# Gate sums from two rounded parts, a per-unit wait in the last stage, and extra products at the third norm

## What is computed

```python
def gla_chunk_scan(q, k, v, log_a, s0):
    def step(s, blk):
        qb, kb, vb, gb = blk
        b = jnp.cumsum(gb, axis=2)          # sums of the tokens' gates
        q_dec = qb * jnp.exp(b)
        att = jnp.where(tri, jnp.einsum('bhtd,bhsd->bhts', q_dec, kb * jnp.exp(-b)), 0.0)
...
log_a = jax.nn.log_sigmoid(z.astype(jnp.float32)) / GLA_TAU
...
h_lat = h_lat + mod_l[2] * o_lat
h_lat = h_lat + mod_l[5] * sqrelu_mlp(modulate(rmsnorm(h_lat, norm2_g[i]), mod_l[3], mod_l[4]),
                                      mlp_w1[i], mlp_w2[i])
...
return rmsnorm(h_lat, final_g)
```

## Time and profile before

| | us |
|---|---|
| executions of the kernel before | 971.64, 972.18, 976.74 |
| their median | 972.18 |
| the profiled execution | 975.54 |
| its span in the profile | 973.7 |
| PE busy / DVE busy / ACT busy | 951.2 / 795.6 / 554.4 |
| mean granted clock of PE, of full speed | 0.994 |

### The profile page before, as it was taken

How to read it: one execution, slowest core, us unless ns; L and a number is a source line. 1 busy time by engine, 2 the same in 40 slices (tenths; PEclk the granted TensorE clock), 3 DMA queues, 4 the chain that set the end, 5 groups by cost and what they waited for, 6 DMA issues and landing times.

```text
span 973.7 us, 20548 instructions
## 1 busy us (share of the span) xinstructions
PE 951.2 (98%) x7196; PEld 913.9 (94%) x7196; DVE 795.6 (82%) x1308; ACT 554.4 (57%) x893; POOL 1.2 (0%) x6
## 2 busy tenths in 40 slices
PE   8999999999999999999999999999999899999996
PEld 7999999999999899999999998888899899998885
DVE  6988899998989789899998987855868777776553
ACT  7445666666455674766666555876533466564432
POOL 0000000000000000000000000000000000000000
PEclk9999999999999999999999999999999989999999
DMA  8876575557767464555557765554673447676651
GB/s 318 271 242 216 171 250 192 189 197 252 258 227 229 161 213 144 184 189 180 182 184 258 241 241 189 183 205 135 228 250 124 136 144 233 225 232 221 193 174 43
DMA packets 53878, 197.27 MB, mean 203 GB/s; under 512 B 5982, under 2 KB 6110, under 8 KB 53696
## 3 DMA queue, kind: packets, MB, share of 16 engines
q1 hardware_dynamic: 53680, 195.49, 60.4%
q10 hardware_dynamic: 144, 1.05, 0.3%
HBM read 195.46 MB, written 1.05 MB: 202 GB/s over the span
## 4 chain that ended last, share of the span: by engine, by line
PE 88%; DVE 7%; ACT 2%; issue 1%; DMA 1%; DVEq 0%; SPq 0%; ACTq 0%
PE ps L474 23%; PE ps L469 20%; PE ps L470 20%; PE ps L473 6%; DVE wlo L1391 3%; PE ps L502 2%; PE ps L504 2%; PE ps L503 2%; ACT whi L894 1%; PE ps L584 1%; PE ps L585 1%; PE ps L586 1%; PE ps L714 1%; PE ps L518 1%; PE ps L450 1%
## 5 line engine op out<-in xcount | busy, mean ns | idle before, releaser
L1391 DVE TENSOR_TENSOR wlo<-raw,whi 128x1024 fp32r<-128x1024 f32 x306 | 370.1, 1219 | 75.5 <-ACT whi L894 74.7
L894 ACT ACTIVATE whi<-raw 128x1024 fp32r<-128x1024 f32 x306 | 320.4, 1053 | 98.4 <-DMA raw<-stream 48.2
L469 PE MATMUL ps<-xhi,whi 128*128 128x256 f32 x1288 | 365.3, 284 | 2.5 <-DVE wlo L1391 0.9
L474 PE MATMUL ps<-xhi,wlo 128*128 128x256 f32 x1288 | 362.6, 281 | 0.0
L470 PE MATMUL ps<-xlo,whi 128*128 128x256 f32 x1288 | 362.6, 281 | 0.0
L469 PEld LDWEIGHTS ps<-xhi,whi 128*128 128x128 f32 x1288 | 244.2, 190 | 4.2 <-DVE wlo L1391 1.5
L470 PEld LDWEIGHTS ps<-xlo,whi 128*128 128x128 f32 x1288 | 244.2, 190 | 0.7 <-issue 0.5
L474 PEld LDWEIGHTS ps<-xhi,wlo 128*128 128x128 f32 x1288 | 244.2, 190 | 0.0
L469 PE MATMUL ps<-yhi,whi 128*128 128x256 f32 x400 | 112.7, 282 | 0.9 <-DVE wlo L1391 0.9
L470 PE MATMUL ps<-ylo,whi 128*128 128x256 f32 x400 | 112.4, 281 | 0.0
L474 PE MATMUL ps<-yhi,wlo 128*128 128x256 f32 x400 | 112.4, 281 | 0.0
(11 more groups left out here) (296 smaller groups left out, 1376.2 us busy)
## 6 DMA issues: line engine op xcount, KB each, us to landing
raw<-stream SPq DMA_DIRECT2D x346, 512.0 KB, 4.1
side<-stream SPq DMA_DIRECT2D x16, 512.0 KB, 4.8
h<-xT SPq DMA_DIRECT2D x2, 512.0 KB, 5.1
c<-ctxT ACTq DMA_DIRECT2D x1, 1024.0 KB, 7.3
ct<-cst SPq DMA_DIRECT2D x1, 962.5 KB, 10.0
rt_tab<-rot SPq DMA_DIRECT2D x1, 896.0 KB
cr<-crow SPq DMA_DIRECT2D x1, 512.0 KB, 7.2
state<-crow SPq DMA_DIRECT2D x1, 512.0 KB, 8.0
```

The source lines that it names most:

```text
L469: pe.matmul(dst, whi[:, w], at(hi, k), start=(k == 0), stop=False)
L474: last = pe.matmul(dst, wlo[:, w], at(hi, k), start=False, stop=(k == K - 1))
L894: c.sig(act.activation(whi[:, s * D:(s + 1) * D], raw[:, r * D:(r + 1) * D], ACT.Copy), hi_ready)
L1391: c.sig(dve.tensor_tensor(wlo[:, w], raw[:, r], whi[:, w], ALU.subtract), slots_done)
```

## The change

- `softplus` of the tokens makes three DVE operations for each direction in place of one: the sum into `za[d]`, its rounded copy `zhi_g[d]` (float32r), and the remainder `zlo_g[d]`. The one of the context stays.
- DVE makes rounded copies of the triangles and of the two-column tables (`sums_r`), once, after the context's `softplus`. All of them are 0, 1 or -1.
- `exponents` makes, instead of each plain float32 product, two float32r products, one with `zhi_g` and one with `zlo_g`, that add up in the same bank.
- In the loop of `mlp_down`, `slot_of_next_unit` counts back from the positions of the second pass: the wait is exact from the second pass on, and in the first pass the first three units wait for one position more than their own.
- `keep_warm(n)` issues n products of `zhi` with itself into bank 5, which nothing reads: 8 ahead of the third norm's column sums (with a wait for bank 5's last reader), 14 behind `spread`.

The new buffers lie over others that are unused at that time.

```diff
@@ -265,18 +265,28 @@
         za = [sb(f"za{d}", GH * T, F32, early) for d in range(2)]
         zm = [sb(f"zm{d}", GH * T, F32, early) for d in range(2)]
         early.close()
+        early = ExitStack()
+        sb("early_held", DC * T + 2 * GH * T, F32, early)
+        zhi_g = [sb(f"zhi_g{d}", GH * T, F32R, early) for d in range(2)]
+        early.close()
         E1 = sb("E1", 2 * GH * T, F32, stage)
         E = [sb("E0", 2 * GH * T, F32, stage), E1]
         qf = [sb(f"qf{d}", GH * T, F32, stage) for d in range(2)]
         gq = sb("gq", GH * T, F32, stage)
         gk = sb("gk", GH * T, F32, stage)
         gv = sb("gv", 2 * D, F32, stage)
+        early = ExitStack()
+        zlo_g = [sb(f"zlo_g{d}", GH * T, F32R, early) for d in range(2)]
+        early.close()
         rsil = sb("rsil", DC * T, F32, stage)
         ki = [sb(f"ki{d}", GH * T, F32, stage) for d in range(2)]
         kz = [sb(f"kz{d}", GH * T, F32, stage) for d in range(2)]
         ck = sb("ck", GH * T, F32, stage)
         kt = sb("kt", GH * T, F32, stage)
         cval = sb("cval", 2 * D, F32, stage)
+        early = ExitStack()
+        sums_r = sb("sums_r", 6 * P + 4, F32R, early)
+        early.close()
         att = sb("att", 2 * 4 * P, F32, stage)
         att_b = sb("att_b", 2 * P, F32, stage)
         osq = sb("osq", 4 * T, F32, stage)
@@ -428,7 +438,10 @@
 
             def slot_of_next_unit():
                 u = c.n.get("unit", 0)
-                pos, step = c.position(u, c.per.get("unit", 0))
+                per = c.per.get("unit", 0)
+                pos, step = c.position(u, per)
+                if per and u >= PHASE_AT["mlp_down"]:
+                    pos, step = POS[u + per] - per, per
                 pe.wait_ge(slots_done, c.i * step + (pos + 1) if step else pos + 1)
                 c.n["unit"] = u + 1
                 return u % RING
@@ -708,15 +721,19 @@
                     pe.wait_ge(ev("expo_read"), n - 2)
                 else:
                     pe.wait_ge(ev("gate_bank_read"), 6)
-                sums = cst_of("sums_b" if d else "sums_f")
+                parts = zhi_g[d], zlo_g[d]
                 for b in range(2):
-                    gates = zm[d][:, b * 512 + m * P:b * 512 + (m + 1) * P]
-                    pe.matmul(ps[5 + n % 3][:, b * T:(b + 1) * T], gates, sums[:, b * P:(b + 2) * P], start=True, stop=True)
-                gates = zm[d][:, d * 512 + m * P:d * 512 + (m + 1) * P]
+                    sums = sums_r[:, (3 * d + b) * P:(3 * d + b + 2) * P]
+                    for i, part in enumerate(parts):
+                        gates = part[:, b * 512 + m * P:b * 512 + (m + 1) * P]
+                        pe.matmul(ps[5 + n % 3][:, b * T:(b + 1) * T], gates, sums, start=(i == 0), stop=(i == 1))
                 if d:
                     pe.wait_ge(ev("factors"), 1)
-                pe.matmul(STAT[:, T + 2 * n:T + 2 * n + 2], gates, cst_of("halves")[:, 2 * d:2 * d + 2], start=True, stop=True)\
-                    .then_inc(ev("expo"), 1)
+                for i, part in enumerate(parts):
+                    gates = part[:, d * 512 + m * P:d * 512 + (m + 1) * P]
+                    last = pe.matmul(STAT[:, T + 2 * n:T + 2 * n + 2], gates, sums_r[:, 6 * P + 2 * d:6 * P + 2 * d + 2],
+                                     start=(i == 0), stop=(i == 1))
+                last.then_inc(ev("expo"), 1)
 
             def ctx_state(d):
                 pe.wait_ge(ev("ctx_keys"), d + 1)
@@ -852,11 +869,19 @@
             gla_out_chunks(2, 4)
             gla_out_chunks(4, 6)
             gla_out_chunks(6, DC)
+            def keep_warm(n):
+
+                for _ in range(n):
+                    pe.matmul(ps[5][:, 0:T], zhi[:, 0:P], zhi[:, 0:T], start=True, stop=True)
+
             units(DC - 3, DC, zhi, zlo)
+            pe.wait_ge(ev("gla_read"), GH)
+            keep_warm(8)
             c.take(ssum_ready, 7)
             pe.wait_ge(ev("n2_square"), 1)
             column_stat_of([ssum[:, 0:T], at(sq, 1)])
             spread()
+            keep_warm(14)
             units(MC, DC, xhi, xlo, chunks=x_ready)
             c.take(y_ready, MC - LATE)
             c.n["y_ready"] += LATE
@@ -1853,7 +1878,12 @@
 
                 i = 2 * n + d
                 dve.wait_ge(ev("gate_ln"), i + 1)
-                dve.tensor_tensor(zm[d][:, :], zm[d][:, :], za[d][:, :], ALU.add).then_inc(ev("softplus"), 1)
+                if n == 0:
+                    dve.tensor_tensor(zm[d][:, :], zm[d][:, :], za[d][:, :], ALU.add).then_inc(ev("softplus"), 1)
+                    return
+                link(dve.tensor_tensor(za[d][:, :], zm[d][:, :], za[d][:, :], ALU.add))
+                link(dve.tensor_copy(zhi_g[d][:, :], za[d][:, :]))
+                dve.tensor_tensor(zlo_g[d][:, :], za[d][:, :], zhi_g[d][:, :], ALU.subtract).then_inc(ev("softplus"), 1)
 
             def ctx_keys(d):
 
@@ -1923,6 +1953,9 @@
                     gate_in_lo(1, 3)
             softplus(0, 0)
             softplus(0, 1)
+            for k, name in enumerate(("sums_f", "sums_b")):
+                dve.tensor_copy(sums_r[:, 3 * k * P:3 * (k + 1) * P], cst_of(name))
+            link(dve.tensor_copy(sums_r[:, 6 * P:6 * P + 4], cst_of("halves")))
             for n in range(2):
                 lo_and_dots(1)
                 final_norm(6 + n)
```

## The result

The changed kernel took 966.82 us (median of 6 runs, 965.41 to 968.77), beside 971.91 us for the kernel before (6 runs, 970.27 to 976.74). The ratio is 0.9949, with a 95% interval of 0.9931 to 0.9968: 0.5% faster. The forecast was 966.5 us, in a range of 963.5 to 970.5. The profiled execution of the changed kernel took 967.01 us, with a span of 965.0 us, against 975.54 and 973.7 before.

The account below looks back on a forecast made before the run. PE was taken to bound the kernel, busy 951.2 of 973.7 us. Gate sums 2.2, third norm 1.9 and last stage 1.6 sum to 5.7 us, taking the median 972.18 to 966.5, range 963.5 to 970.5.

Parts of the forecast that it names:

- The step from the profile's sum to the median: Whole kernel: the profiled execution lies 3.4 us above the median, unexplained, so 5.7 us come off the median 972.18 too.
- Gate sums, PE's work: Eight calls of `exponents`: each falls from 1.05 to 0.61 us, so PE's work shrinks by 3.55 us.
- Gate sums, DVE: Softplus of the tokens: sum 1.22, cast 0.72, subtraction 1.22 us per direction; PE's first call starts 0.6 us later.
- Gate sums, ACT: Fourth call: PE stands 0.85 us for ACT, whose table load follows its wait for direction 1; 2.2 us gained overall.
- The tables: Three casts after the context's softplus, at most 0.5 + 0.5 + 0.2 us, cost nothing; without cover 1.2.
- The third norm: Unread products around sums and spread keep the clock at 2.4 GHz: 1.9 us gained, plus or minus 0.25.
- The last stage: Exact wait in `mlp_down`: 1.6 us gained in the last pass; first-pass loss between 0 and 0.1, taken as 0.
- the gates give little: Rival at the gate sums: DVE and ACT bound there, gain 0.6 to 1.2 instead of 2.2, 968 us; chance 0.17.
- the clock falls anyway: Rival at the third norm: PE cold, 14 products take 3.0 us, gain 0.2 instead of 1.9, 968.2 us; chance 0.13.
- the cast is slow: Rival at the gate sums: a cast takes 7 us, PE stands for it, 979.1 us, slower than before; chance 0.03.
- the wait is moved to the first pass: Rival in `mlp_down`: the first pass pays what the last one saves, 968.1 us; chance 0.05.

Follow-up runs that it names:

- undo_gates: The changed kernel with the plain float32 products and one-step softplus of before, without the table casts: 969.0 us, ratio 0.995 to the kernel before.
- before_again: The kernel before, unchanged, run again for a second profile: 972.82 us for one run, beside 973.75 (11 runs).
- undo_warm: The changed kernel without its 22 unread products: 969.33 us (10 runs), ratio 0.9958 to the kernel before.
- warm8_only: The changed kernel without the 14 unread products behind the spread, keeping the 8 ahead of the column sums: 971.97 us, one run.
- warm14_only: The changed kernel without the 8 unread products ahead of the column sums, keeping the 14 behind the spread: 972.61 us, one run.

## Why the prediction was right, and where it was wrong

**The whole.** 5.7 us were forecast. The two pairs of profiles show 5.96 and 5.70 us at the three places, and no new wait but the 0.1 us at the start of `mlp_down`. Between medians it is 5.1 and 4.6 us. The forecast for the median, 966.5, came close to the 966.82 of the first comparison, and 969.11 in the second shows how much of that is luck. The step from the profile's sum to the median, that nothing in an execution explains why it lies above or below, holds for the two profiles of each kernel: they differ mainly by the distance between products in stages that the change doesn't touch.

**Gate sums, PE's work.** Forecast 0.61 us a call, 3.55 saved. The eight calls take 5.43 us in all (11.96 less 5.78 for V6 and V7 and 0.75 ahead of the first), 0.68 each, so 8.43 - 5.43 = 3.00 us are saved. The small products themselves cost little more than the 0.12 us assumed for the two (0.14 us, 657.68 to 657.82). What was put at nothing is the first full product behind them: its successor comes 0.20 us later (657.82 to 658.02) instead of 0.12, in the five calls that follow another call. In the first call, behind its wait, it is 0.22.

**Gate sums, DVE.** Forecast 0.72 us for the cast, 0.69 measured. The extrapolation from one-source operations of 128 and 256 elements held at 1024. The first call waits 0.52 us, forecast 0.6. The table casts took 0.36, 0.36 and 0.17 us (at most 0.5, 0.5 and 0.2).

**Gate sums, ACT: the failed step.** Forecast was a wait of 0.85 us at the fourth call, since the first `decays` "waits for direction 1: 662.1, signal 0.1, then the table load of 1.28 us, which stood behind this wait". It doesn't stand behind it. In the rows before, load and exponential followed one another, and the wait ahead of the load was for PE's call, because direction 1 had long been ready; they could not tell where a later wait for direction 1 would fall. In the changed kernel the load is done during that wait, direction 1 is in use at 660.20, two exponentials are over some 0.9 us later, 661.1, and the fourth call at 662.02 needs nothing. Two smaller slips are in the same passage: it takes V6 at 2.8 us, where its own row gives 2.89, so that the wait would be some 0.8; and the terms listed for ACT add up to 664.35, not 664.5. So the forecast of 2.2 us came about by two errors of opposite sign: 0.55 too much saved on PE, and a wait of 0.8 that wasn't there. That it lies near the measured 2.48, which is 3.00 less 0.52, is luck in part.

**The tables** were free, as forecast: the three casts take 0.7 us together (624.22 to 624.93), and PE waits for nothing between 622 and 656 us.

**The third norm.** Forecast 1.9 us: 0.26 from the spread and what follows it, the rest from products at full clock. Measured 1.88, with 0.25 and 1.64. The clock stays at 2.4 GHz, the 14 end 0.17 us ahead of the first chunk (forecast 0.1), and the chunks of `xlo` set the pace. The Trainium skill ("TensorE: Matmul & The Clock Gate", Part 1) has the moment of the rise vary by half a microsecond between runs, by which I gave the term plus or minus 0.25. The runs agree on the size. In the three profiles without the groups the rise comes 4.33, 3.28 and 4.04 us behind the first product of the pair, a spread of 1.05 us. The stretch is then 13.46, 13.20 and 13.59 us, and 11.57 to 11.60 with the groups, so the gain lies between 1.6 and 2.0.

**The last stage.** Forecast 1.6 us and nothing paid in the first pass, with a bound of 0.1. Measured 1.60, and undone 1.61, but as 1.7 less 0.1: the prediction left out that the product behind a wait is followed late as well, in the last pass where it is gained and in the first where it is paid.

**The rivals.** That the gates give little falls with 2.48 us and `undo_gates`; but the place is as sensitive to DVE as it assumed: 2.8 us of casts more cost 2.1. That the clock falls anyway falls with the window at 1.00; with either half alone it came true in the one profile of each. With the 14 alone it came as described: they take 3.13 us and hold up the first chunk. That the cast is slow falls with 0.69 us. That the wait is moved to the first pass is true of 0.1 us, and falls for the rest with 90.61 us for the stage.

## What to carry to other kernels

Where the hardware scatters by as much as an edit is worth, price edits between fixed marks on the bounding engine's timeline: there three undone parts gave 2.5, 1.6 to 2.0 and 1.6 us, to be told apart with one profile each, where medians could not separate them. Unread products kept the clock up here when they filled both pauses of the stretch; in one profile each, filling one of two brought nothing. They are free only as long as the wait they fill. When new work is put ahead of a wait, ask of each instruction behind it whether it waits itself or only stands behind one that does: a table load that doesn't wait for the data hides in the wait.

## What the runs showed of the hardware that I had not expected

- **The pace of one and the same stage has several values.** With float32r products of 256 columns back to back, a full granted clock and no wait, the mean distance between neighbours over 77 us was 117.3, 117.4, 118.7 or 120.0 ns, and both kernels show more than one. `mlp_up` shows it too, 84.5 or 85.44 us for the same products. This is most of what the two profiles of one kernel differ by (2.70 us for the kernel before, 2.38 for the changed one). On two chips four profiles of different kernels agreed in the window of 30 to 107 us, on a third they did not. Its cause is open; the DMA rate in these windows, 241 to 245 GB/s, hardly differs, and is a result of the pace as well as it could be a reason.
- **The low stretch of the clock had one length.** In all five profiles where it fell at the third norm it stayed at 1.2 GHz for 6.83 us (before 777.94 to 784.77, before_again 775.67 to 782.50, undo_warm 774.13 to 780.96, warm8_only 776.84 to 783.66, warm14_only 775.09 to 781.92). What PE did meanwhile differed: with the 14 unread products it worked through nearly all of it, without them it paused for 1.8 us. The clock fell 2.3 to 4.5 us after the last full product and rose 1.9 to 5.8 us after the first of the pair. The prediction's rival had reckoned the rise from the start of steady work, 4.3 us behind it; that is no constant.
- **A table load can run ahead of the wait of its own activation** (658.04 against 660.20, and 661.70 against 665.31 with more casts).
- **The first full product behind a break is followed late.** Behind products of two columns it is 0.20 us instead of 0.12. Behind a wait it is 0.22 instead of 0.12 (657.10 to 657.32), and with 512 columns 0.33 instead of 0.23 (866.42 to 866.75). So a wait cost 0.1 us here beyond the delay of the product that waited.
